# Two pairs of each FFN as plain block products, prompt values by pairs of heads, and raw weights issued ahead of past loads

## The chip, the cores and the metric

One core of a Trainium2 chip runs one launch. The metric is device microseconds (us) of that launch. TensorE (PE) multiplies matrices, VectorE (DVE) and ScalarE (ACT) work elementwise, GpSimd (POOL) makes one kind of operand, and SyncE (SP) issues most of the DMAs.

## The reference

One inference step of two layers of a streaming encoder over 640 tokens: 512 of a prompt and 8 sequences of 16 "sample" tokens with 256 cached past rows each. Width 1024, FFN width 2816.

```
for each of the 2 layers (s, b, g come from a conditioning vector, "ada"):
  x += 0.5*(1+g1) * SwiGLU1(rmsnorm(x)*(1+s1)+b1)
  n  = rmsnorm(x)*(1+s2)+b2
  x += (1+g2) * concat(GLA(n @ W_in), MLA(n @ W_in)) @ W_out
  x += 0.5*(1+g3) * SwiGLU2(rmsnorm(x)*(1+s3)+b3)
swiglu(x): a, b = split(x @ w_in); (silu(a) * b) @ w_out
MLA: 8 heads, scores over a low-rank latent of 256 and a rotary key of 32, block-causal softmax, values of 64 per head
```

GLA is gated linear attention of 4 heads. The last step is one more rmsnorm.

## The kernel before

**Arithmetic.** An fp32 operand is split into a high part (a cast to fp32r, on ACT) and the rest (`lo`, a subtraction on DVE or POOL), and a product is three matmul passes: high by high, weight high by token low, weight low by token high. Tokens run in two halves of 320 columns (`cols`). The small matmuls of the attention are plain fp32; each of them shows as two passes in the trace.

**FFN.** Its 2816 hidden columns are 22 *pairs* (128 columns of the gate, 128 of the up matrix), in three portions of 8, 8 and 6 pairs, each followed by its part of the output matrix (`ffn`, PE L1050). A pair and its tokens are seen as 2x2 blocks (gate or up by input half; input half by token half) and are multiplied by a scheme of **seven block products** in place of eight. One block product (`product`, L1040) is 4 chunks by 3 passes = 12 passes of 320 columns on lines L1045, L1046 and L1047. With two layers of two FFNs there are 4 x 22 pairs x 7 x 12 = 7392 such passes. The scheme needs

- token operands: the blocks B11, B21, B22 of the normed input, and four sums T_1 to T_4 of blocks (`tsum` on DVE), each cast on ACT (`hi`, L600) and subtracted on DVE (`lo`, L1587);
- weight operands: three raw blocks and four sums `s_t`, two made early (`s_in_pair`) and two later (`s_late`, L1722) on DVE, with casts on ACT (`hi_a` to `hi_d`, L519, L534, L524, L529) and `lo` on DVE (`lo_a` to `lo_d`);
- sums of results: copies out of PSUM on ACT (`half_out` L618 with L622, L641, L656) and additions on DVE, with SiLU on ACT.

An FFN starts behind the last residual of the stage before it. Then come, in order: the last squares (`tail` on DVE), the norm's `rstd` with a load of the SiLU table (L577), scaling (`scaled`, DVE) and bias (L596, ACT), the casts and residuals of B11 and B21, the four sums with theirs, and B22. The function is `norm_hi_t` (L589) on ACT and `norm_apply_t` (L1562) on DVE. The weights of the first pair are prepared ahead of this by `first_hi` and `first_lo`.

**Mixer.** `mix_pe` (L1126), `mix_act` (L694), `mix_dve` (L1804). Its 28 + 8 weight units of 512 KB come through two `raw` buffers, are cast by `feed(k)` on ACT (L695, cast L514) into four `w_hi` slots, and POOL makes `w_lo` (L479). The attention is one software-pipelined loop of 40 steps: 8 sample steps (one sequence each), then 32 prompt steps (8 heads by 4 query tiles `qt`, head by head). A step is: scores (PE L1429), a maximum (DVE L2092), an exponential (ACT L926 and, for samples, L928), a normalisation (DVE L2106), transposes (PE L1441), a copy out of PSUM (ACT), values (`values`, L1444: PE L1458 for samples, L1468 for the prompt). Prompt values of one head are 64 output rows; even heads fill rows 0 to 63 of a bank, odd heads rows 64 to 127. L1486 multiplies the sample latents by `w_uv`, 64 rows per head.

**What sets the order.** Every engine has its own program written out in order; engines meet only at semaphores. ACT waits for a raw unit's DMA inside `feed`; SP issues the units in order, each when `w_lo` of an earlier unit is done, and puts the loads of past keys and values (`load_past`, L410) between them at unit `U_UV`.

Of the kernel before, what the change touches and what calls it, by code (L numbers as in the profile page):

```python
# [11 lines left out]
P = 128  # L12
# [17 lines left out]
WPL = 6 * DC + MIX_U  # L30
# [17 lines left out]
B11, B21, T_2, T_1, T_3, T_4, B22 = range(7)  # L48
# [28 lines left out]
def build(nc, xT, cT, lng, bada, fing, selc, wmain, wada, scanm, gk2_in, gains_in, tri_in, bd_in, seqm_in,  # L77
          ident_in, qmask_in, kmask_in, cs_in, ukT, wuv_in, past_kT, past_v, past_pe, s0_in,
          y_out, ckv_out, kpe_out, glap_out, glas_out):
    with ExitStack() as ctx:  # L80
# [60 lines left out]
        t_hi = [sb(f"t_hi{i}", [P, 4, HALF], F32R, at=a)[0] for i, a in enumerate(tok_at)]  # L141
        t_lo = [sb(f"t_lo{i}", [P, 4, HALF], F32R, at=a + 5120)[0] for i, a in enumerate(tok_at)]
        n32 = sb("n32", [P, DC, NT], at=arena_a)[0]
        t_two = sb("t_two", [P, 4, HALF], at=arena_a + 20480)[0]
# [44 lines left out]
        pt_p = [in_a(f"pt_p{i}", [P, 4, P], 30720 + 2048 * i) for i in range(3)]  # L189
# [111 lines left out]
        pv_mm = signal("pv_mm", 32)  # L301
# [76 lines left out]
        def whole(l, f, p, m):  # L378
            return l * WPL + f * (3 * DC + MIX_U) + p * DC + m

        def mixw(l):
            return l * WPL + 3 * DC

# [3 lines left out]
        def pairs_next(l, f, p):  # L387
            return p < 2 or (f == 1 and l + 1 < DEPTH)

        def pair(l, f, p, c):  # L390
            return (l * 2 + f) * NFF + PBASE[p] + c

# [4 lines left out]
        SBANKS, TBANKS = (6, 5, 2, 3), (7, 0)  # L397

# [7 lines left out]
        def _(sp):  # L406
# [34 lines left out]
            for l in range(DEPTH):  # L441
                for f in range(2):
                    for p in range(3):
                        n0, w0 = pair(l, f, p, 0), whole(l, f, p, 0)
                        for c in range(PORT[p]):
                            if f == 0:
                                for k in range(2):
                                    load_ada(4 * ada_block(l, p, c) + 2 * (c % 2) + k, k, 2)
                            sp.wait_ge(s_step, 4 * (n0 + c) + 4)
                            for k in range(2):  # L450
                                load_main(unit(l, f, p, 2 * c + 2 + k))
# [23 lines left out]
        def _(pool):  # L475
# [24 lines left out]
            for l in range(DEPTH):  # L500
                for first, count in ((0, 28), (28, WPL - 28)):
                    if first:
                        norm_samples(l)
                    with pool.Fori(0, count // 4) as i:
# [5 lines left out]
        def _(act):  # L510
# [59 lines left out]
            def norm_rstd(g, s):  # L570
# [5 lines left out]
                if s and g < 3 * DEPTH:  # L576
                    act.preload_act_table_set(WITH_SILU)  # L577
# [11 lines left out]
            def norm_hi_t(g, gi):  # L589

                def bias(i):
                    h, half = i % 2, i // 2
                    c = (slice(0, HALF), slice(HALF, SEQ))[half]
                    act.wait_ge(xr_done, 4 * gi + i + 1)
                    for m in range(4 * h, 4 * h + 4):
                        act.activation(n32[:, m, c], n32[:, m, c], ACT.Identity, bias=mod_b[:, m, 0:1],  # L596
# [4 lines left out]

                act.wait_ge(mab_done, 2 * g + 2)
                for h in range(2):
                    bias(h)
                    act.wait_ge(nb_done, 16 * gi + 4 * h + 4)
                    hi((B11, B21)[h], n32[:, 4 * h:4 * h + 4, cols[0]])
                bias(2)
                bias(3)
                half_out(NFF * gi)
                for i, need, src in ((T_2, 2, t_two[:]), (T_1, 1, n32[:, 0:4, cols[0]]), (T_3, 3, n32[:, 0:4, cols[1]]),  # L610
                                     (T_4, 4, n32[:, 4:8, cols[0]])):
                    act.wait_ge(tsum_done, 4 * gi + need)
                    hi(i, src)
                act.wait_ge(nb_done, 16 * gi + 16)
                act.wait_ge(sam_step, 3 * gi + 3)
                hi(B22, n32[:, 4:8, cols[1]])
# [7 lines left out]
            def ffn(l, f):  # L624
                for p in range(3):
                    n0, w0, last = pair(l, f, p, 0), whole(l, f, p, 0), PORT[p] - 1
                    for c in range(PORT[p]):
                        n = n0 + c
                        if c == 0 and p:
                            half_out(n)  # L630
                        act.wait_ge(p2_mm, n + 1)
                        if c < last:
                            hi_a(n + 1, unit(l, f, p, 2 * c + 2))
                        else:
                            split_hi(w0, unit(l, f, p, 2 * PORT[p]))
                        act.wait_ge(c11_done, n + 1)
                        act.activation(g0[n % 2][:], g0[n % 2][:], ACT.Silu).then_inc(sil_done, 1)
                        act.wait_ge(p6_mm, n + 1)
# [1678 lines left out]
```

## Time and profile before

| | |
|---|---|
| median of 3 runs | 2818.18 us (2817.44 to 2822.74) |
| the profiled execution | 2817.91 us, its span 2815.8 us |
| mean granted TensorE clock in the span | 0.963 |
| PE busy | 2607.1 us, 93% |
| DVE busy | 1588.2 us, 56% |
| ACT busy | 1085.9 us, 39% |
| POOL busy | 407.4 us, 14% |
| DMA | 283.86 MB, mean 101 GB/s |

The span is the time in the trace from the first to the last instruction of the core; 2.1 us of the execution lie outside it. A granted clock of 1.00 is 2.4 GHz and 0.50 is 1.2 GHz. Rows name buffers without their numbers; `<-` stands between outputs and inputs, and the text in brackets at the end of a timeline row is the idle time of the engine just before the instruction and what ended it. A row with `x8` is a run of eight like instructions with their common duration.

### The profile page before, as it was taken

What the parts mean: (1) busy time and instruction counts of PE and PEld (TensorE: products, weight loads), DVE (VectorE), ACT (ScalarE), POOL (GpSimd) and SP (SyncE); (2) the same over time, 40 slices, a digit from 0 to 9 for tenths busy, and PEclk for the clock granted to TensorE, in tenths of its full rate; (3) what the DMA queues carried; (4) which work ended last, traced back from release to release, by engine and by line L of the source; (5) the groups of instructions that cost most, each with busy time, mean ns of one, the idle gap of its engine ahead of it and who ended that gap; (6) DMA issues with size and microseconds to landing.
All of it is one profiled execution on the core that took longest, in us unless ns stands there. A gap on an engine that the chain in (4) does not pass through costs nothing.

```text
span 2815.8 us, 42934 instructions
## 1 busy us (share of the span) xinstructions
PE 2607.1 (93%) x17236; PEld 2417.7 (86%) x17236; DVE 1588.2 (56%) x2712; ACT 1085.9 (39%) x1844; POOL 407.4 (14%) x170
## 2 busy tenths in 40 slices
PE   5799999989889979999979999998998897999997
PEld 1499999989786869999969999998987686999997
DVE  2573655553654476473767466466257437747474
ACT  1342433432444254252454334244334435525242
POOL 0002020233220101102110201114321010020202
PEclk8899999989989989999989999998999998999998
DMA  8543443422240112122224334242215101222222
GB/s 324 211 150 105 135 134 107 135 80 75 71 156 15 33 58 94 58 91 74 98 71 146 119 122 143 98 142 84 87 38 161 51 31 37 92 68 90 76 88 85
DMA packets 81759, 283.86 MB, mean 101 GB/s; under 512 B 10048, under 2 KB 13024, under 8 KB 80928
## 3 DMA queue, kind: packets, MB, share of 16 engines
q1 hardware_dynamic: 75168, 263.81, 27.4%
q10 hardware_dynamic: 6400, 17.37, 2.1%
q8 instruction: 136, 2.23, 0.3%
q14 instruction: 55, 0.45, 0.1%
HBM read 274.69 MB, written 6.46 MB: 100 GB/s over the span
## 4 chain that ended last, share of the span: by engine, by line
issue 69%; PE 20%; POOL 9%; DVE 1%; ACT 1%; POOLq 0%; DMA 0%; DVEq 0%; ACTq 0%
POOL w_lo L479 8%; PE bank L1045 3%; PE bank L1047 3%; PE bank L1046 3%; PE bank L1003 2%; PE bank L1005 2%; PE bank L1004 2%; PE bank L1468 1%; PE bank L1429 1%; PE bank L1458 0%; PE bank L1441 0%; DVE t_lo L1587 0%; DVE y_sb L2173 0%; PE bank L1415 0%; DVE h_lo L1772 0%
## 5 line engine op out<-in xcount | busy, mean ns | idle before, releaser
L1045 PE MATMUL bank<-t_hi,w_hi 128*128 128x320 f32 x2464 | 781.5, 317 | 69.9 <-DVE t_lo L1587 49.8
L1046 PE MATMUL bank<-t_lo,w_hi 128*128 128x320 f32 x2464 | 769.0, 312 | 0.0
L1047 PE MATMUL bank<-t_hi,w_lo 128*128 128x320 f32 x2464 | 768.9, 312 | 0.0
L479 POOL TENSOR_TENSOR w_lo<-raw,w_hi 128x1024 fp32r<-128x1024 f32 x160 | 394.0, 2467 | 2371.2 <-ACT w_hi L514 2371.2
L1045 PEld LDWEIGHTS bank<-t_hi,w_hi 128*128 128x128 f32 x2464 | 469.9, 191 | 118.7 <-issue 60.6
L1046 PEld LDWEIGHTS bank<-t_lo,w_hi 128*128 128x128 f32 x2464 | 470.7, 191 | 0.0
L1047 PEld LDWEIGHTS bank<-t_hi,w_lo 128*128 128x128 f32 x2464 | 470.0, 191 | 0.0
L1003 PE MATMUL bank<-h_hi,w_hi 128*128 128x320 f32 x1408 | 436.3, 310 | 1.4 <-DVE h_lo L1772 1.0
L1004 PE MATMUL bank<-h_lo,w_hi 128*128 128x320 f32 x1408 | 435.1, 309 | 0.0
L1005 PE MATMUL bank<-h_hi,w_lo 128*128 128x320 f32 x1408 | 435.1, 309 | 0.0
L514 ACT CAST w_hi<-raw 128x1024 fp32r<-128x1024 f32 x160 | 166.9, 1047 | 317.3 <-PE bank L1005 283.3
L1003 PEld LDWEIGHTS bank<-h_hi,w_hi 128*128 128x128 f32 x1408 | 264.3, 188 | 3.3 <-DVE h_lo L1772 3.3
L1004 PEld LDWEIGHTS bank<-h_lo,w_hi 128*128 128x128 f32 x1408 | 264.3, 188 | 0.0
L1005 PEld LDWEIGHTS bank<-h_hi,w_lo 128*128 128x128 f32 x1408 | 264.3, 188 | 0.0
L1664 DVE SCALAR_TENSOR_TENSOR x<-bank,mod_g,x 128x192 f32<-128x192 f32 x112 | 46.8, 418 | 283.2 <-PE bank L1005 283.1
L1003 PE MATMUL bank<-n_hi,w_hi 128*128 128x320 f32 x448 | 142.0, 317 | 19.3 <-DVE n_lo L1635 19.3
L524 ACT CAST w_hi<-s_t 128x1024 fp32r<-128x1024 f32 x88 | 92.2, 1048 | 162.4 <-DVE s_t L1714 100.3
L1659 DVE SCALAR_TENSOR_TENSOR x<-bank,mod_g,x 128x320 f32<-128x320 f32 x112 | 61.5, 549 | 151.6 <-PE bank L1005 151.6
L1004 PE MATMUL bank<-n_lo,w_hi 128*128 128x320 f32 x448 | 141.0, 315 | 0.0
L1005 PE MATMUL bank<-n_hi,w_lo 128*128 128x320 f32 x448 | 141.0, 315 | 0.0
L1759 DVE TENSOR_TENSOR up<-up,bank 128x320 f32<-128x320 f32 x88 | 43.0, 488 | 155.6 <-ACT up L656 155.6
L529 ACT CAST w_hi<-s_t 128x1024 fp32r<-128x1024 f32 x88 | 92.4, 1050 | 95.9 <-PE bank L1005 51.4
(263 smaller groups left out, 4103.0 us busy)
## 6 DMA issues: line engine op xcount, KB each, us to landing
raw<-in_wmain SPq DMA_DIRECT2D x336, 512.0 KB, 3.6
araw<-in_wada SPq DMA_DIRECT2D x144, 512.0 KB, 4.6
x<-in_xT SPq DMA_DIRECT2D x1, 2560.0 KB, 15.1
pk_t<-in_pastkT SPq DMA_DIRECT2D x10, 256.0 KB, 4.3
pv<-in_pastv SPq DMA_DIRECT2D x10, 256.0 KB, 5.0
y<-y_sb SPq DMA_DIRECT2D x1, 2560.0 KB, 7.5
s_s<-in_s ACTq DMA_DIRECT2D x4, 512.0 KB, 5.1
uk_t<-in_ukT ACTq DMA_DIRECT2D x2, 1024.0 KB, 6.2
```

Of the source, the lines that this page charges most:

```text
L479: pool.tensor_tensor(w_lo[slot][:], raw[slot % 2][:].rearrange("p (c m) -> p c m", m=P), w_hi[slot][:].bitcast(F32), ALU.subtract).then_in ...
L514: act.copy(w_hi[w % 4][:], raw[at % 2][:].rearrange("p (c m) -> p c m", m=P)).then_inc(whi_done, 1)
L524: act.copy(w_hi[1][:], s_t[:]).then_inc(hib_done, 1)
L529: act.copy(w_hi[3][:], s_t[:]).then_inc(hic_done, 1)
L1003: pe.matmul(out, w_hi[w][:, c, :], r_hi, start=first, stop=False)
L1004: pe.matmul(out, w_hi[w][:, c, :], r_lo, start=False, stop=False)
L1005: return pe.matmul(out, w_lo[w][:, c, :], r_hi, start=False, stop=last)
L1045: pe.matmul(out, hi, t_hi[i][:, c, :], start=first and c == 0, stop=False, skip_group_check=True)
L1046: pe.matmul(out, hi, t_lo[i][:, c, :], start=False, stop=False, skip_group_check=True)
L1047: mm = pe.matmul(out, lo, t_hi[i][:, c, :], start=False, stop=(c == 3), skip_group_check=True)
L1659: dve.scalar_tensor_tensor(out=x[:, m, cols[0]], in0=y0[:, 0:HALF], scalar=mod_g[:, m, 0:1], in1=x[:, m, cols[0]], op0=ALU.mult, op1=ALU.a ...
L1664: dve.scalar_tensor_tensor(out=x[:, m, HALF:SEQ], in0=y1[:, 0:HP1], scalar=mod_g[:, m, 0:1], in1=x[:, m, HALF:SEQ], op0=ALU.mult, op1=ALU.add)
```

## The change

1. **Plain pairs.** `PL = 2`: the first two pairs of each FFN are multiplied as eight block products each (`straight`), first both pairs for tokens 0 to 319, then both for tokens 320 to 639. They take B11, B21, B12 and B22 and raw weights (four units cast by `split_hi`, subtracted by `low_plain`), and no sums. B12 becomes a token block of its own; T_4 lies in B12's place and is cast when the plain products are done. The sums T_1 to T_4 and the operands of the third pair are made while the plain products run. SiLU reads PSUM, and so does the multiplication by the up part (`up_mul`).
2. **Norm.** The SiLU table is loaded behind the cast of B21; `tail(0)` stands ahead of the first scaling.
3. **Feeds and loads.** Of the four units that `feed` cast between the latent queries and the attention loop, two are cast before that, ahead of the `w_uv` step, and two in loop steps 5 and 6. SP issues two more raw units ahead of the past loads.
4. **Prompt values.** The loop takes the heads in pairs, alternating the two heads at each `qt`. `values` runs every second step for both heads, and successive matmuls go to rows 0 to 63 and 64 to 127 in turn; `w_uv` (L1486) alternates in the same way. `pt_p` has four buffers in place of three.

```diff
-B11, B21, T_2, T_1, T_3, T_4, B22 = range(7)
+B11, B21, B12, B22, T_2, T_1, T_3, T_4 = range(8)
+T_HOME = (0, 1, 3, 6, 2, 4, 5, 3)
...
+        def prompt_tile(it):
+            j = it - NDEC
+            return 2 * (j // 8) + j % 2, (j % 8) // 2
...
-                            if k == U_UV:
+                            if k == U_OUT:
                                 sp.wait_ge(gla_st, 64 * l + 64)
                                 load_past(l, (0, 1))
+                            elif k == U_OUT + 1:
                                 sp.wait_ge(wslot_free, mixw(l) + U_UK + 4)
                                 load_past(l, (2, 3, 4))
...
+                act.preload_act_table_set(WITH_SILU)
...
+                silu(1, 1)
+                act.wait_ge(wslot_free, pl + 8)
+                hi_sum(T_4, 4, n32[0][:, 4:8, :])
+                next_hi(2)
+                h_high(1, 1)
+                next_hi(3)
...
+                feed(20)
+                feed(21)
...
-                for k in range(20, 24):
-                    feed(k)
...
+                    if it in (5, 6):
+                        feed(17 + it)
...
+                    if p == 0:
+                        for s in range(2):
+                            for c in range(PL):
+                                straight(c, s, 0)
+                                straight(c, s, 1)
...
+                    if it % 2 == 0:
+                        return
...
                     for k in range(qt + 1):
-                        mm = pe.matmul(bank[(4, 1)[hp % 2]][r0:r0 + MV, qt * P:(qt + 1) * P],
-                                       v_m[:, k, h * MV:(h + 1) * MV], pt_p[it % 3][:, k, :], start=(k == 0), stop=(k == qt))
+                        for e in range(2):
+                            mm = pe.matmul(bank[(4, 1)[hp % 2]][MV * e:MV * e + MV, qt * P:(qt + 1) * P],
+                                           v_m[:, k, (2 * hp + e) * MV:(2 * hp + e + 1) * MV],
+                                           pt_p[(it - 1 + e) % 4][:, k, :], start=(k == 0), stop=(k == qt))
...
-                tail(0)
...
+                dve.wait_ge(nb_done, 16 * gi + 16)
                 tsum(0, n11, n12, n11)
+                up_mul(0, 0)
                 tsum(1, t_two[:], n22, n11)
+                h_low(0, 0)
```

**Order on ACT at the start of the first FFN, before** (`t_hi0` and `t_hi1` are the casts of B11 and B21, `t_hi2` to `t_hi5` of the sums, `t_hi6` of B22; L622 is the copy out of PSUM that the third product waits for):

```order
L577 ACT_TABLE_LOAD
L596 ACTIVATE n32_102<-n32_102,mod_b_75,mod_a_74 128x320 x4
L600 CAST t_hi0_88<-n32_102 128x1280
L596 ACTIVATE n32_102<-n32_102,mod_b_75,mod_a_74 128x320 x4
L600 CAST t_hi1_89<-n32_102 128x1280
L596 ACTIVATE n32_102<-n32_102,mod_b_75,mod_a_74 128x192 x8
L622 COPY g0_0_118<-bank0 128x320
L600 CAST t_hi2_90<-t_two_103 128x1280
L600 CAST t_hi3_91<-n32_102 128x1280
L600 CAST t_hi4_92<-n32_102 128x1280
L600 CAST t_hi5_93<-n32_102 128x1280
L600 CAST t_hi6_94<-n32_102 128x1280
```

and **now** (the end of the plain part on ACT: L639 is SiLU from PSUM, L643 the cast of a finished hidden column, `t_hi7` the cast of T_4, `w_hi0` to `w_hi3` those of the third pair, L685 the copy that was L622):

```order
L639 ACTIVATE g1_0_123<-bank0 128x320
L541 CAST w_hi0_56<-raw0_54 128x1024
L643 CAST h_hi_52<-g1_0_123 128x320
L546 CAST w_hi1_57<-s_t_120 128x1024
L639 ACTIVATE g1_1_124<-bank1 128x320
L622 CAST t_hi7_95<-n32_0_104 128x1280
L556 CAST w_hi2_58<-raw1_55 128x512
L643 CAST h_hi_52<-g1_1_124 128x320
L551 CAST w_hi3_59<-s_t_120 128x1024
L685 COPY g0_0_121<-bank0 128x320
```

The casts of the sums now stand among the SiLUs of the plain pairs, and the copy out of the first product by sevens stands behind the cast of T_4 and both late weight casts.

**Order on ACT at the start of the attention of layer 0, before** (L910 copies the latent queries, L514 are the four feeds, L926 and L928 the first exponential):

```order
L910 COPY q_abs_137<-bank3 128x4x8x16
L514 CAST w_hi0_56<-raw0_54 128x1024
L514 CAST w_hi1_57<-raw1_55 128x1024
L514 CAST w_hi2_58<-raw0_54 128x1024
L514 CAST w_hi3_59<-raw1_55 128x1024
L926 ACTIVATE p_s0_139,psums_85<-bank6,mx_84 128x256
```

and **now** (the same place; L1004 copies transposed scores out of PSUM, L945 and L951 issue loads of past rows):

```order
L971 COPY q_abs_140<-bank3 128x4x8x16
L984 ACTIVATE p_s0_142,psums_85<-bank6,mx_84 128x256
...
L1004 COPY pt_s1_147<-bank0 128x384
L536 CAST w_hi2_58<-raw0_54 128x1024
L951 DMA pv1_193<-in_pastv 128x512
L984 ACTIVATE p_s2_144,psums_85<-bank2,mx_84 128x256
L986 ACTIVATE p_s2_144,psum2_86<-bank2,mx_84 128x16
L1004 COPY pt_s0_146<-bank7 128x384
L536 CAST w_hi3_59<-raw1_55 128x1024
```

No feed stands any longer between the latent queries and the first exponential; two stand behind the copies of steps 5 and 6.

**Order on PE in the prompt attention, before** (L1441 transposes, L1468 values of one head into `bank4`, L1429 scores):

```order
L1441 MATMUL bank7<-ident_82,p_p2_172 128x128 x3
L1468 MATMUL bank4<-pt_p0_147,v_m_136 64x128 x2
L1429 MATMUL bank5<-k_h_167,q_h_166 128x256
```

and **now** (L1544, L1575 and L1532 are the same three):

```order
L1544 MATMUL bank7<-ident_82,p_p0_174 128x128 x3
L1575 MATMUL bank4<-pt_p2_152,v_m_139 64x128
L1575 MATMUL bank4<-pt_p3_153,v_m_139 64x128
L1575 MATMUL bank4<-pt_p2_152,v_m_139 64x128
L1575 MATMUL bank4<-pt_p3_153,v_m_139 64x128
L1532 MATMUL bank3<-k_h_171,q_h_170 128x512
L1544 MATMUL bank0<-ident_82,p_p1_175 128x128 x3
L1532 MATMUL bank6<-k_h_171,q_h_170 128x128
```

Values stand in every second step, twice as many at a time, with `pt_p` of the two heads in turn.

## Rows read from the trace of the kernel before

**Rows 1.** part 1 of the page, the kernel before: busy time of each engine
```profile
PE 2607.1 (93%) x17236; PEld 2417.7 (86%) x17236; DVE 1588.2 (56%) x2712; ACT 1085.9 (39%) x1844; POOL 407.4 (14%) x170
```

**Rows 2.** stretches (start:end, us, busy of PE, PEld, DVE, ACT, POOL, PEclk, DMA, GB/s)
```profile
109.90:152.10 42.20, 36.23 (x216) 33.55 (x217) 36.06 (x42) 24.16 (x38) 0.00 (x0) 0.86 0.30 99
998.40:1041.40 43.00, 33.87 (x193) 32.97 (x194) 35.83 (x41) 24.17 (x38) 0.00 (x0) 0.87 0.12 35
1458.70:1503.60 44.90, 37.24 (x216) 34.56 (x217) 37.31 (x44) 24.19 (x38) 0.00 (x0) 0.84 0.29 93
2350.50:2393.50 43.00, 33.47 (x192) 32.57 (x193) 35.82 (x42) 24.22 (x38) 0.00 (x0) 0.88 0.11 36
```

**Rows 3.** timeline of PE, FFN start 1 (start, duration, operation, [idle before])
```profile
109.92 0.64 PE L1045 MATMUL bank<-t_hi,w_hi 128*128 128x320 f32 x1 [7.92 <-DVE t_lo L1587]
...
113.40 0.63 PE L1045 MATMUL bank<-t_hi,w_hi 128*128 128x320 f32 x1
...
130.76 0.31 PE L1045 MATMUL bank<-t_hi,w_hi 128*128 128x320 f32 x1
...
132.52 0.31 PE L1045 MATMUL bank<-t_hi,w_hi 128*128 128x320 f32 x1
```

**Rows 4.** the stretches again: half speed after one short wait
```profile
1480.30:1483.70 3.40, 3.40 (x14) 3.40 (x14) 2.48 (x5) 1.37 (x2) 0.00 (x0) 0.50 0.01 4
```

**Rows 5.** timeline of DVE, first residual at FFN starts 1 and 2
```profile
108.37 1.49 DVE L1587 TENSOR_TENSOR t_lo<-n,t_hi 128x1280 fp32r<-128x1280 f32 x1
...
996.90 1.49 DVE L1587 TENSOR_TENSOR t_lo<-n,t_hi 128x1280 fp32r<-128x1280 f32 x1 [2.57 <-ACT t_hi L600]
```

**Rows 6.** groups of instructions: count, busy, mean ns, idle before
```profile
L1722 DVE TENSOR_TENSOR s_t<-raw,s_t 128x512 f32<-128x512 f32 x88 | 60.2, 684 | 0.0
...
L622 ACT COPY g<-bank 128x320 f32<-128x320 f32 x88 | 37.4, 425 | 87.6 <-PE bank L1047 87.6
...
L1587 DVE TENSOR_TENSOR t_lo<-n,t_hi 128x1280 fp32r<-128x1280 f32 x24 | 35.0, 1487 | 12.1 <-ACT t_hi L600 12.1
...
L600 ACT CAST t_hi<-n 128x1280 fp32r<-128x1280 f32 x24 | 29.4, 1257 | 8.9 <-DVE n L1592 8.6
```

**Rows 7.** timelines of DVE, ACT and PE, start of the attention, layer 0
```profile
825.98 0.44 DVE L2092 TENSOR_REDUCE mx<-bank 128x1 f32<-128x272 f32 x1 [2.54 <-PE bank L1422]
...
830.79 1.04 ACT L514 CAST w_hi<-raw 128x1024 fp32r<-128x1024 f32 x1 [5.17 <-DMA raw<-in_wmain]
...
834.34 0.47 ACT L926 ACTIVATE p_s<-bank,mx 128x256 f32<-128x256 f32 x1
...
837.57 0.69 PE L1441 MATMUL bank<-ident,p_s 128*128 128x128 f32 x2 [7.70 <-DVE p_s L2106]
```

**Rows 8.** who waited for whom: us in total, times, longest
```profile
PE bank L1441 <- DVE p_s L2106: 15.2, 2, 7.7
```

**Rows 9.** the stretches again: after the wait at the attention's start
```profile
831.70:845.40 13.70, 7.83 (x31) 7.29 (x32) 4.71 (x14) 4.98 (x20) 4.68 (x2) 0.50 0.52 170
```

**Rows 10.** tile of the past keys, layer 0 (min/median/max, first and last issue)
```profile
L415 SPq DMA_DIRECT2D pk_t<-in_pastkT x5: 328/427/433, 792.1 to 811.2; - x5
...
DMA to landing us min/median/max: 2.6/4.3/6.8
```

**Rows 11.** timeline of PE in the prompt attention
```profile
871.33 2.02 PE L1486 MATMUL bank<-o_lat,w_uv 128*64 128x128 f32 x32
...
898.95 1.09 PE L1468 MATMUL bank<-pt_p,v_m 128*64 128x128 f32 x8
...
902.47 0.55 PE L1441 MATMUL bank<-ident,p_p 128*128 128x128 f32 x3 [0.38 <-DVE p_p L2106]
...
909.94 0.55 PE L1441 MATMUL bank<-ident,p_p 128*128 128x128 f32 x3 [0.38 <-DVE p_p L2106]
```

**Rows 12.** groups of instructions: passes of the prompt values
```profile
L1468 PE MATMUL bank<-pt_p,v_m 128*64 128x128 f32 x320 | 48.3, 282 | 3.2 <-DVE o_lat L2110 3.2
```

**Rows 13.** the stretches again: four rounds of the prompt attention
```profile
882.50:912.40 29.90, 28.38 (x154) 18.02 (x153) 16.09 (x49) 15.07 (x50) 0.00 (x0) 1.00 0.00 1
```

More of the change, by code:

```diff
@@ L443, in _ @@
                     for p in range(3):
-                        n0, w0 = pair(l, f, p, 0), whole(l, f, p, 0)
+                        n0, w0 = seven(l, f, p, 0), whole(l, f, p, 0)
                         for c in range(PORT[p]):
+                            straight = c < first_pair(p)
+                            for k in range(2):
+                                if straight:
+                                    sp.wait_ge(wlo_done, plain(l, f) + 2 * c + k + 1)
+                                    load_main(unit(l, f, p, 2 * c + 2 + k))
                             if f == 0:
@@ L605, in norm_hi_t @@
                     act.wait_ge(nb_done, 16 * gi + 4 * h + 4)
[L606 to L613, printed above, removed]
+                    hi((B11, B21)[h], n32[0][:, 4 * h:4 * h + 4, :])
+                if gi == 0:
+                    for k in range(2, 2 * PL):
+                        split_hi(k, k)
+                act.preload_act_table_set(WITH_SILU)
+                for h in range(2):
+                    bias(2 + h)
                 act.wait_ge(nb_done, 16 * gi + 16)
                 act.wait_ge(sam_step, 3 * gi + 3)
-                hi(B22, n32[:, 4:8, cols[1]])
+                for h in range(2):
+                    hi((B12, B22)[h], n32[1][:, 4 * h:4 * h + 4, :])
+                silu(0, 0)
+                hi_sum(T_2, 2, t_two[:])
+                h_high(0, 0)
+                hi_sum(T_1, 1, n32[0][:, 0:4, :])
+                silu(1, 0)
+                hi_sum(T_3, 3, n32[1][:, 0:4, :])
+                h_high(1, 0)
+                silu(0, 1)
+                next_hi(0)
+                h_high(0, 1)
+                next_hi(1)
+                silu(1, 1)
[4 more added lines that the diff above has]
+                next_hi(3)
             def half_out(k):
@@ L626, in ffn @@
                     n0, w0, last = pair(l, f, p, 0), whole(l, f, p, 0), PORT[p] - 1
-                    for c in range(PORT[p]):
-                        n = n0 + c
-                        if c == 0 and p:
+                    for c in range(first_pair(p), PORT[p]):
+                        n, k = n0 + c, seven(l, f, p, c)
+                        if c == first_pair(p):
                             half_out(n)
@@ L983, in _ @@
                 last_square(0, s, None)
[L984 to L985 removed]
+            for k in range(2):
+                split_hi(k, k)
             for s in range(2):
@@ new lines, in straight @@
+                    def straight(c, s, up):
+                        n, slot = n0 + c, 2 * c + up
+                        b = (BW, BY)[c] if up else BZ[c]
+                        pe.wait_ge(wlo_done, pl + slot + 1)
+                        if s:
+                            if up:
+                                pe.wait_ge(hf0_done, n + 1)
+                            else:
+                                pe.wait_ge(sil_done, 2 * n0 + c + 1)
+                        elif up:
+                            pe.wait_ge(y_free, 4 + 2 * out_tile(l, f, 0, 0))
+                        elif n >= 2:
+                            pe.wait_ge(hf0_done, n - 1)
+                        for h in range(2):
+                            i = ((B11, B21), (B12, B22))[s][h]
+                            if c == 0 and not up:
+                                tokens(i)
+                            mm = product(slot, 4 * h, i, b, h == 0)
+                        mm.then_inc(wslot_free if s else (p2_mm if up else p1_mm), 1)
@@ L1072, in ffn @@
+                    for c in range(first_pair(p), PORT[p]):
+                        n, k = n0 + c, seven(l, f, p, c)
+                        new = p == 0 and c == PL
                         z = BZ[n % 2]
-                        if c == 0:
-                            tokens(B11)
-                            one(n)
-                            tokens(B21)
+                        if c == first_pair(p):
+                            one(c)
                             pe.wait_ge(y_free, 4 + 2 * out_tile(l, f, p, 0))
-                            two(n)
```

355 lines of the change are left out of this document (217 added, 138 removed).

## The prediction

> **What bounds the kernel.** I read the busy times first: PE works 93% of the span and no other engine more than 56% [rows 1]. So a microsecond is won where PE is idle, where its clock is at the lower level, or where it does work it need not do. The stretches around each FFN's start show the first two: 42 to 45 us long, the granted clock on the mean 0.84 to 0.88 [rows 2]. The timeline there shows the pace: a product took 3.48 us at the start (109.92 to 113.40) and 1.76 us later (130.76 to 132.52) [rows 3]: 1.2 and 2.4 GHz. The waits show a third place: PE waits twice, 15.2 us together, for the first normalised scores of the attention [rows 8], and is at half clock behind it [rows 9]. In the prompt attention the clock is full and PE busy for 28.38 of 29.9 us, so there only less PE work, or work that overlaps better, helps [rows 13].
>
> **The sum** is made against the profiled execution, 2817.91 us with a span of 2815.8; that is 0.27 below the median of the runs, which is nothing here (what a measurement of this kernel can tell from no change is about 0.2%, 5.6 us).
>
> **FFN starts.** Each stretch of rows 2 holds 16 products of 12 passes (192 passes; 216 where 24 ada passes run too). At 1.76 they take 28.2 us. The second and fourth stretch take 43.0, an excess of 14.8 each. In the first, PE is idle for 42.20 - 36.23 = 6.0 and loses at most 42.2 x 0.14 = 5.9 by its clock; some idle time counts twice, so I take 11. In the third it is 7.7 and at most 7.2: I take 14. The changed kernel also runs 16 products there, but they stand for two pairs where sevens need 14. So, per start:
>
> - *Removed*: the whole excess (11, 14.8, 14, 14.8), since B11 and B21 suffice for the first eight products and B12 and B22 are wanted only 14 us later.
> - *Earlier start*: DVE waited 2.57 us for the cast of B21 at start 2, not at all at start 1 [rows 5]; all such waits are 12.1 [rows 6]. With the table load behind that cast I take 2.3 at starts 2 to 4 and 0 at start 1.
> - *Added*: two products, 24 passes, 3.5 us at full clock.
> - *Left*: PE still starts at half clock. One beginning as long as the stretch of [rows 4], 3.40, loses 1.7; with the ramp's waits for B21 I take 2.1.
> - *A new wait*. T_4's cast waits for the end E of the plain products. ACT and DVE run in order, so behind it come: cast 1.26, `lo` 1.49, a weight residual and two `s_late` at about 0.68 each, a cast of 128x1024 (1.04 in [rows 7]), the copy out of PSUM 0.43 [rows 6]. That is 6.3, with the semaphores about 6.7. Only then may the third product by sevens start, and PE has two products (3.5) to cover it: **3.2 us** of idle time, 2.4 in the FFNs that have ada work there. The T_3 product then waits some 1.1 (0.2 with ada work), since its SiLU and copy are queued behind a weight cast whose raw unit is issued only after `s_late`.
> - *Clock*: a stretch of 3.40 us at 0.50 [rows 4] followed one short wait in the kernel before. I count one such loss per start for the new waits, 1.5, a little under half of 3.40 since part of it lies in the wait.
>
> Sums: start 1: 11 - 3.5 - 2.1 - 2.4 - 0.2 - 1.5 = 1.3. Start 2 and 4: 14.8 + 2.3 - 3.5 - 2.1 - 3.2 - 1.1 - 1.5 = 5.7. Start 3: 14 + 2.3 - 3.5 - 2.1 - 2.4 - 0.2 - 1.5 = 6.6. Together **19**. Bounds: without new waits and clock loss 19 + 2 x 5.8 + 2 x 4.1 = 39; with twice the idle time and clock loss about -1. I stay at 19, since each link of the chain has a row.
>
> Costed at nothing: the up multiplication and SiLU from PSUM (each has a product's time of 3.5 us or more to its next use); the three subtractions of raw weights that replace `s_t` work (DVE is 56% busy; at FFN 1 two units more are cast inside the norm, where ACT waits for DVE anyway); POOL's work, which is unchanged.
>
> **Start of the attention.** The first maximum is ready at 825.98 + 0.44 = 826.4. ACT could take the exponential then, but is in front of the third and fourth feed: 5.17 us for a raw unit's DMA, the casts, and the exponential starts at 834.34 [rows 7]. That is 7.9 late, and PE's wait for its consumer is 7.70. With no feed there, the wait goes, and nothing else is late: the same engine order reaches the exponential as soon as the maximum is there. Behind the wait stands a stretch of 13.7 us at 0.50 with 7.83 of PE work [rows 9]; at full clock that is 3.9 less. So 7.6 + 3.9 = 11.5 per layer, **23** in two. Bounds: 15 (the clock falls all the same, by the waits of the sample steps) and 25. The two feeds now stand in steps 5 and 6, where their raw units have had several steps to land, and cost ACT 1.04 each beside PE work; if the cast were late, the maximum of the following step would wait a microsecond. SP issues the past loads behind two more raw units. Even if all were issued only at 811.2, where the last one stands now, and took the longest landing, 6.8 [rows 10], they are there at 818.0, ahead of the scores that end at 825.98. So nothing.
>
> **Prompt values in pairs.** Eight passes of one head took 1.09, the last one's own 0.28 counted in: a pitch of 0.115. The 32 passes that go to both column halves took 2.02: a pitch of 0.056 [rows 11, 12]. Two heads need 40 passes per eight steps, so at most 2.4 us are won, 2.2 with the ends of shorter groups. Half as many groups save perhaps 0.4 in ends. Two waits of 0.38 for the normalised scores (902.47 and 909.94, one per period) may go: 0.76. A period of four steps is 7.47 now [rows 11], eight are 14.94. PE's work would be 14.94 - 3.3 = 11.6. The softmax chain of a step then has less time, and with DVE at 16.09 and ACT at 15.07 per 16 steps [rows 13] they are not full, but in-order waits give back some; I take 1.4. 13.0 against 14.94, four times per layer: 7.8, **16** in two. Bounds: 0 (the chain sets the period) and 26. `w_uv` already runs at 0.056: nothing.
>
> 19 + 23 + 16 = 58: **2760 us**, a span near 2757.5.
>
> A rule that speaks against the third part stands in the Trainium skill, page "TensorE: Matmul & The Clock Gate", section "Part 3: Packing small matmuls": a weight load overlaps matmuls in flight only if its row group differs, and two column halves share all rows. By it no pass would overlap the other half's. The page "TensorEngine Tiling (Array Packing)", section "Key Properties", has tiles load and multiply in parallel. The trace, with 0.056 per pass in two halves against 0.115 in one, agrees with the latter so far.
>
> **Rivals.**
>
> (a) *The FFN starts give nothing*: the wait on T_4's chain is longer than I have it (a raw unit that lands late, a clock that stays low), and eats the 19. For it: the chain has seven links on two engines in order. Against: every link has its row. 2779.
>
> (b) *Pairing gives nothing*: the softmax chain bounds the loop, or the halves of two different moving operands don't overlap. For: the PE waits of 0.38 exist already. Against: DVE and ACT are about half idle. 2776.
>
> (c) *Better*: the sums' chain is covered, and no clock loss follows it. 2740.
>
> (d) *Slower: alternating halves serialise*, so that each pass takes its own mean 0.282 [rows 12]. Prompt values: 320 x (0.282 - 0.115) = 53. `w_uv`: 64 x (0.282 - 0.056) = 14. With the 16 lost: 2760 + 83 = 2843. It decides from a pitch at which 42 us (the other two parts) are eaten: (42 - 14)/320 + 0.115, about 0.20. Against: the rows of `w_uv`, where halves change every four passes. This is what the rule of "Part 3: Packing small matmuls" in the Trainium skill's page "TensorE: Matmul & The Clock Gate" would make of the change.
>
> (e) *The feeds are only moved*: the scores of steps 5 and 6 wait for raw units as step 0 did, so that the wait goes on there and only the clock is better: 2760 + 15 = 2775.
>
> **Chances.** Forecast as worked 0.62; (a) 0.11, (b) 0.09, (c) 0.08, (e) 0.04; (d) 0.04; 0.02 for two or more of the first failures together, near no change. The range takes in (a), (b), (e) and (c): 2740 to 2786, where the upper end is (a) and part of a second failure, and leaves out some 0.1 to 0.15. Faster by over 0.2%: all but (d) and the last: 0.93. Within 0.2%: 0.02. Slower: 0.05, (d) and a little.
>
> **What the profile would show.** Right: 7392 + 96 = 7488 product passes; no PE wait of 7.7 on normalised scores, and ACT not waiting on a raw DMA ahead of the first exponential; prompt-value passes at a pitch near 0.056 and a period of eight steps near 13.0; at each FFN start no waits on `t_lo` but the first, and a new one of 2.4 to 3.2 on the copy out of PSUM (L685) with a fall of the clock behind it. Wrong: a pitch above 0.11 or a period above 14.5 (b, d); new waits of 6 us or more behind the plain products (a); a wait on raw units within the sample steps (e).

## The result, and the profile after

The changed kernel takes **2749.04 us** (median of 4 runs, 2740.86 to 2751.49) beside 2820.38 (2817.44 to 2822.74, 4 runs): a ratio of 0.9742, 95% interval 0.9718 to 0.9767. The forecast was 2760, its range 2740 to 2786. The profiled execution took 2751.49 us, its span 2749.7, so the two profiles stand 66.1 us apart; the sums below are made against that.

Part 1 of the page of the changed kernel, to be held against [rows 1]:

```profile
PE 2584.8 (94%) x17332; PEld 2406.6 (88%) x17332; DVE 1545.5 (56%) x2644; ACT 1068.9 (39%) x1808; POOL 407.8 (15%) x170
```

PE has 96 passes more and is still busy 22 us less: the values overlap, and less of the time is at half clock (157 us, for 212). The rest of the 66 us is idle time that has gone. I divide both traces at the same places of the program: the first pass of an FFN, the last pass of its eighth pair, the first pass on `n_hi` (mixer), the first score of the attention and the first pass on `o_hi` (the output projection). A boundary is the start of the pass that it names.

| stretch | before | after | gain |
|---|---|---|---|
| start to the first FFN | 109.92 | 104.12 | 5.8 |
| FFN starts, 8 pairs each | 122.36, 114.59, 125.01, 114.59 | 121.24, 109.67, 121.48, 109.73 | 14.4 |
| ends of FFN 1 and 3 to the mixer's first pass | 53.77, 53.75 | 52.03, 52.02 | 3.5 |
| mixer up to the attention | 227.96, 228.03 | 227.47, 227.52 | 1.0 |
| attention | 106.04, 106.00 | 87.03, 86.91 | 38.1 |
| to the start of FFN 2, 3 and 4 | 68.58, 56.94, 69.21 | 67.90, 53.54, 67.90 | 5.4 |
| all else, the end among it | | | -2.1 |

The last row has a place. From the eighth pair of FFN 4 to the end the changed kernel takes 2.4 more, and PE's waits there are two that the kernel before does not have at that place: 1.11 at 2643.2 (L704, behind a cast that waited 1.28 for its raw unit) and 0.96 at 2690.0 (for `h_lo`). No run tests where they come from.

**FFN starts.** The stretches of the changed kernel (columns as in [rows 2]) from the first pass up to the end of the 18 products ahead of T_2, at starts 1 and 2, and the half-clock stretch behind start 2's new wait:

```profile
104.12:141.70 37.58, 37.58 (x240) 35.27 (x240) 29.16 (x31) 21.05 (x30) 0.00 (x0) 0.93 0.25 85
969.58:1003.18 33.60, 33.60 (x216) 33.09 (x216) 26.27 (x26) 19.56 (x28) 0.00 (x0) 0.95 0.05 17
...
1007.20:1010.60 3.40, 3.40 (x15) 3.40 (x14) 1.24 (x3) 2.22 (x4) 0.00 (x0) 0.50 0.48 195
```

216 passes, 18 products, took 33.60 us with PE busy throughout; before, 16 products took 43.0. Then comes the forecast wait, in the waits of the changed kernel (who waited for whom, us in total, times, longest). The wait on L704 is the one at 2643.2, not at a start.

```profile
PE bank L1107 <- ACT g L685: 9.9, 4, 2.9
...
PE bank L1107 <- ACT g L704: 1.1, 1, 1.1
```

The timelines of ACT and DVE show the chain behind T_4's cast at start 2, link by link as the prediction has it; ACT's 2.74 of waiting is DVE's four links:

```profile
999.70 1.27 ACT L622 CAST t_hi<-n 128x1280 fp32r<-128x1280 f32 x1 [1.62 <-PE bank L1109]
1000.88 0.61 ACT L556 CAST w_hi<-raw 128x512 fp32r<-128x512 f32 x1
1001.40 0.46 ACT L643 CAST h_hi<-g 128x320 fp32r<-128x320 f32 x1
1004.59 1.04 ACT L551 CAST w_hi<-s_t 128x1024 fp32r<-128x1024 f32 x1 [2.74 <-DVE s_t L1867]
1005.54 0.42 ACT L685 COPY g<-bank 128x320 f32<-128x320 f32 x1
```
```profile
1001.01 1.49 DVE L1693 TENSOR_TENSOR t_lo<-n,t_hi 128x1280 fp32r<-128x1280 f32 x1 [0.75 <-ACT t_hi L622]
1002.42 0.69 DVE L1847 TENSOR_TENSOR w_lo<-raw,w_hi 128x512 fp32r<-128x512 f32 x1
1003.21 0.69 DVE L1866 TENSOR_TENSOR s_t<-raw,raw 128x512 f32<-128x512 f32 x1
1003.82 0.68 DVE L1867 TENSOR_TENSOR s_t<-raw,s_t 128x512 f32<-128x512 f32 x1
```

**Attention.** The first exponential of layer 0 is released by DVE's maximum and no longer follows a cast; PE's wait of 7.7 [rows 7, 8] is gone (ACT's timeline, the waits, and PE's timeline of one period):

```profile
817.27 0.47 ACT L984 ACTIVATE p_s<-bank,mx 128x256 f32<-128x256 f32 x1 [2.72 <-DVE mx L2249]
```
```profile
PE bank L1544 <- DVE p_s L2263: 0.6, 2, 0.3
```
```profile
865.96 0.55 PE L1544 MATMUL bank<-ident,p_p 128*128 128x128 f32 x3 [0.90 <-DVE p_p L2263]
866.44 0.66 PE L1575 MATMUL bank<-pt_p,v_m 128*64 128x128 f32 x8
...
869.60 0.66 PE L1544 MATMUL bank<-ident,p_p 128*128 128x128 f32 x4 [0.89 <-DVE p_p L2263]
870.19 0.88 PE L1575 MATMUL bank<-pt_p,v_m 128*64 128x128 f32 x12
...
872.90 1.09 PE L1575 MATMUL bank<-pt_p,v_m 128*64 128x128 f32 x16 [0.25 <-ACT pt_p L1011]
...
879.31 0.55 PE L1544 MATMUL bank<-ident,p_p 128*128 128x128 f32 x3 [0.91 <-DVE p_p L2263]
```

The same 320 passes, which kept PE busy for 48.3 before [rows 12], keep it busy for 24.5, each with the mean of 282 ns that it had:

```profile
L1575 PE MATMUL bank<-pt_p,v_m 128*64 128x128 f32 x320 | 24.5, 282 | 2.5 <-ACT pt_p L1011 2.2
```

Sixteen passes take the 1.09 that eight took in [rows 11]. With the last one's 0.28 taken off that is (1.09 - 0.28) / 15 = 0.054 per pass. A period of eight steps is 879.31 - 865.96 = 13.35, against 2 x 7.47 before; two waits of 0.9 per period, and smaller ones, stand where two of 0.38 were.

**What no step of the prediction had.** The first FFN starts 5.8 us earlier. PE's timeline shows where: its wait for the first `ev` in the prologue was 11.28 before, and is 4.48 now.

```profile
41.55 1.88 PE L1024 MATMUL bank<-sel,ev 128*128 128x9 f32 x8 [11.28 <-DVE ev L1541]
```
```profile
34.70 1.88 PE L1086 MATMUL bank<-sel,ev 128*128 128x9 f32 x8 [4.48 <-DVE ev L1647]
```

DVE's timeline shows what stood ahead of that `ev`, before (the last of the first pair's weight residuals) and now (the two residuals of raw units):

```profile
39.66 1.23 DVE L1697 TENSOR_TENSOR w_lo<-s_t,w_hi 128x1024 fp32r<-128x1024 f32 x1 [1.17 <-ACT w_hi L529]
40.81 0.68 DVE L1541 COPY ev<-bank 128x512 f32<-128x512 f32 x1
```
```profile
31.48 2.56 DVE L1886 TENSOR_TENSOR w_lo<-raw,w_hi 128x1024 fp32r<-128x1024 f32 x2 [0.21 <-ACT w_hi L536]
33.96 0.68 DVE L1647 COPY ev<-bank 128x512 f32<-128x512 f32 x1
```

And at the mixer's start PE waits 4.6 in place of 6.3 for the first `n_lo` (waits, before and after):

```profile
PE bank L1003 <- DVE n_lo L1635: 19.3, 6, 6.3
```
```profile
PE bank L1065 <- DVE n_lo L1780: 14.6, 4, 4.6
```

### The profile page after: what moved, and what is told of

Same layout as the page of the kernel before. It is cut to its first block and busy times, and to the rows that moved or that the text cites. A ratio compares the mean times of both kernels' runs of the same rounds, so it can differ in the third digit from the quotient of the medians.

```text
span 2749.7 us, 42964 instructions
## 1 busy us (share of the span) xinstructions
PE 2584.8 (94%) x17332; PEld 2406.6 (88%) x17332; DVE 1545.5 (56%) x2644; ACT 1068.9 (39%) x1808; POOL 407.8 (15%) x170
## 5 line engine op out<-in xcount | busy, mean ns | idle before, releaser
L1109 PE MATMUL bank<-t_hi,w_lo 128*128 128x320 f32 x2496 | 777.1, 311 | 0.0
L1108 PE MATMUL bank<-t_lo,w_hi 128*128 128x320 f32 x2496 | 776.9, 311 | 0.0
L536 ACT CAST w_hi<-raw 128x1024 fp32r<-128x1024 f32 x176 | 183.3, 1046 | 340.0 <-PE bank L1067 323.5
L546 ACT CAST w_hi<-s_t 128x1024 fp32r<-128x1024 f32 x80 | 83.8, 1048 | 145.7 <-DVE s_t L1859 97.8
L551 ACT CAST w_hi<-s_t 128x1024 fp32r<-128x1024 f32 x80 | 83.9, 1049 | 99.1 <-PE bank L1067 51.4
```

The costliest lines, as they stand in the source:

```text
L536: act.copy(w_hi[w % 4][:], raw[at % 2][:].rearrange("p (c m) -> p c m", m=P)).then_inc(whi_done, 1)
L546: act.copy(w_hi[1][:], s_t[:]).then_inc(hib_done, 1)
L551: act.copy(w_hi[3][:], s_t[:]).then_inc(hic_done, 1)
L1108: pe.matmul(out, hi, t_lo[i][:, c, :], start=False, stop=False, skip_group_check=True)
L1109: mm = pe.matmul(out, lo, t_hi[i][:, c, :], start=False, stop=(c == 3), skip_group_check=True)
```

## The experiments

Eight kernels, seven from the changed one and one from the kernel before. Stretches are those of the table above.

### The attention's parts alone

```diff
 # the kernel before, with:
+ prompt_tile, values by pairs, four pt_p, pv_mm of 16, w_uv in turns
+ feed(20), feed(21) ahead of w_uv; feed(22), feed(23) in steps 5 and 6
+ past loads at U_OUT and U_OUT + 1
```

> The kernel before with parts 3 and 4 of the change alone (feeds and past loads, prompt values in pairs); FFNs, norm and prologue as before. My theory (the parts add up; in the changed kernel's profile the attention is 19 us shorter per layer): 38 us under the kernel before, so about 2780, with FFN starts as before. Rival (the attention gains only because something ahead of it, in the FFN or the mixer's start, hands over earlier): less than 30 us, 2790 or more.

Measured: 2785.95 (2784.03 to 2787.71), ratio 0.9879, 0.9863 to 0.9896. The attention takes 86.88 in both layers, as in the changed kernel, and the FFN starts are the old ones within 1.6 (122.35, 114.55, 123.46, 115.50). The attention alone gives 38.3. The time is 34 less, between the 38 of the theory and the 30 of its rival: two stretches beside the attention grew (from the attention to FFN 2 70.67 for 68.58, the second mixer 230.33 for 228.03), and each has a stretch of 3.4 us at half clock that the kernel before does not have there. So the attention's gain needs nothing of the FFNs, and a little of it is given back. Half the total, 34 of 71, is this; the FFNs, the prologue and the mixer's start are the other half. No run separates, within the FFN starts, the plain pairs from the new order of the norm (part 2).

### The four feeds in front of the loop again

```diff
-                feed(20)
-                feed(21)
...
+                for k in range(20, 24):
+                    feed(k)
                 for it in range(40 + 6):
...
-                    if it in (5, 6):
-                        feed(17 + it)
```

> The changed kernel with all four feeds in front of the attention loop again; SP's order of loads stays the new one. My theory (ACT's in-order wait for raw units ahead of the first exponential cost the 7.6 us and the half clock behind it): PE waits 7 to 8 us for the first normalised scores again in each layer, a stretch of 10 to 14 us at half clock behind it, and the kernel is 20 to 24 us slower than the changed one, about 2771. Rival (the gain came from SP's earlier raw units, which stay): the wait is under 3 us and the kernel within 6 us of the changed one.

Measured: 2766.39 (2764.87 to 2769.11), 17 above the changed kernel. The wait is back, and so is the half clock (waits, and the stretch behind the one in layer 0):

```profile
PE bank L1542 <- DVE p_s L2261: 15.3, 2, 7.7
```
```profile
823.50:837.20 13.70, 8.33 (x32) 7.70 (x33) 4.71 (x14) 4.85 (x19) 4.34 (x2) 0.50 0.48 164
```

ACT again stands 5.04 us in front of a raw unit:

```profile
822.03 1.04 ACT L536 CAST w_hi<-raw 128x1024 fp32r<-128x1024 f32 x1 [5.04 <-DMA raw<-in_wmain]
```

The attention takes 98.25 and 96.05: 11.2 and 9.1 more. The order on ACT is the cause; SP's earlier raw units, which this kernel keeps, do not remove the wait. In layer 1 the half-clock stretch was 6.8 long and not 13.7, which goes with the difference between the two layers. The sum of 20.3 lies in the 20 to 24 expected, the total of 17 does not: among the stretches without an edit, the way to FFN 2 and the start of FFN 3 are 1.5 and 1.8 shorter here.

### One head after the other

```diff
-            return 2 * (j // 8) + j % 2, (j % 8) // 2
+            return j // 4, j % 4
...
-                    if it % 2 == 0:
-                        return
...
-                        for e in range(2):
-                            mm = pe.matmul(bank[...][MV * e:MV * e + MV, ...], ..., pt_p[(it - 1 + e) % 4][:, k, :], ...)
+                        e = h % 2
+                        mm = pe.matmul(bank[...][MV * e:MV * e + MV, ...], ..., pt_p[it % 4][:, k, :], ...)
```

> The changed kernel with the prompt's heads one after the other and values of one head per step, four buffers kept. My theory (overlap of the two column halves): four steps take 7.4 to 7.5 us again, a pass 0.11 in place of 0.054; the kernel is 12 to 16 us slower than the changed one, about 2763. Rival (the period comes from the softmax chain, not from the values): within 4 us of the changed kernel.

Measured: 2766.23 (2757.79 to 2767.32), 17 above the changed kernel. The attention takes 94.90 in both layers, 7.9 and 8.0 more. The rows of four steps are those of [rows 11] again, 877.76 - 870.29 = 7.47 apart:

```profile
870.29 0.55 PE L1544 MATMUL bank<-ident,p_p 128*128 128x128 f32 x3 [0.38 <-DVE p_p L2261]
...
874.24 1.09 PE L1573 MATMUL bank<-pt_p,v_m 128*64 128x128 f32 x8
...
877.76 0.55 PE L1544 MATMUL bank<-ident,p_p 128*128 128x128 f32 x3 [0.38 <-DVE p_p L2261]
```

7.9 here and 11.2 for the feeds make 19.1, the 19.0 that the attention of layer 0 gained: there the two add up. In layer 1 they make 17.1 of 19.1, since the half-clock stretch that came back with the feeds was the shorter one. The medians differ by 17, one more than the 12 to 16 expected; the two profiled executions differ by only 6.3, since this kernel's ran with fewer stretches at half clock (a mean granted clock of 0.976, against 0.972 in its other three). So the 7.9 of the attention is the measure here, and not the total.

### Pairs, but one half's matmuls behind the other's

```diff
-                    for k in range(qt + 1):
-                        for e in range(2):
+                    for e in range(2):
+                        for k in range(qt + 1):
```

> The changed kernel with the values of a pair of heads in another order: all of one head's matmuls, then all of the other's, in place of turns. Theory A (halves overlap only if neighbours in the order go to different halves): a group of 16 passes takes 1.5 to 1.7 us in place of 1.09, and the period of eight steps grows by 1 to 2 us. Theory B (a run of one half can run ahead beside the other's, as the passes of w_uv did in the kernel before, which changed halves every four passes at 0.056 each): the group of 8 stays at 0.66 to 0.75, that of 16 below 1.3.

One run: 2758.18. Neither theory holds for all lengths (PE's timeline):

```profile
880.81 0.67 PE L1575 MATMUL bank<-pt_p,v_m 128*64 128x128 f32 x8
884.56 1.15 PE L1575 MATMUL bank<-pt_p,v_m 128*64 128x128 f32 x12
887.54 1.58 PE L1575 MATMUL bank<-pt_p,v_m 128*64 128x128 f32 x16 [0.25 <-ACT pt_p L1011]
```

In turns these are 0.66, 0.88 and 1.09. Two runs of 4 passes overlap as fully as turns do; of two runs of 6 or 8 only a part lies side by side. A period is 14.10 (13.35 in turns), 0.75 more and not the 1 to 2 of theory A. The attention takes 89.80 and 89.68, 2.8 more in each layer: of the 7.9 that pairing gives, 2.8 come from the turns. PE's busy time on these passes is 48.3 with single heads, 30.6 here and 24.5 in turns.

### A longer prologue

```diff
+            dve.wait_ge(whi_done, 1)
+            for k in range(5):
+                dve.tensor_tensor(s_t[:], raw[0][:]..., w_hi[0][:].bitcast(F32), ALU.subtract).then_inc(put_back, 1)
+                dve.wait_ge(put_back, k + 1)
             for k in range(2):
                 low_plain(k)
```

> The changed kernel with five more subtractions of 128x1024 on DVE ahead of the two weight residuals of the prologue, into a buffer that is free there (about 6.5 us of work that nobody needs). My theory (the 5.8 us that the first FFN starts earlier come from the three weight residuals, four sums and two waits that DVE no longer does ahead of the first ada result): PE's wait for that result grows from 4.5 to about 11 us, the first FFN starts 5 to 6.5 us later, and the kernel is 5 to 6.5 us slower, about 2755. Rival (the ada weights' loads set the prologue's end): the start stays within 1.5 us.

Measured: 2753.01 (2748.54 to 2756.16). PE's wait is long again, and the first FFN starts at 108.78, 4.7 later:

```profile
40.41 1.88 PE L1087 MATMUL bank<-sel,ev 128*128 128x9 f32 x8 [10.77 <-DVE ev L1648]
```

That is a little under the 5 to 6.5 expected, and far from the rival's 1.5: by the place where the FFN starts the mechanism holds. In the six kernels that have this prologue and no edit in it, the changed one among them, that place lies between 102.46 and 104.12. The medians lie 4.0 apart, which is less than either kernel's own spread, so the total alone would not have told.

### The cast behind the second rstd again

```diff
                                 last_square(g, 1, out_tile(l, f, 2, m))
+                                if f == 0:
+                                    norm_rstd(g, 1)
...
-                    if p == 2:
+                    if p == 2 and f == 1:
                         norm_rstd(g, 1)
```

> The changed kernel with the cast of a raw unit on ACT behind the second half's rstd and the table load at the mixer's start again, as in the kernel before, in place of ahead of it. My theory (that place delays the mixer's first operand): PE's wait for the first n_lo grows from 4.6 to 6.3 us in each layer, the half-clock stretch from 13.7 to 17.1, and the kernel is 4 to 6 us slower, about 2754. Rival (other parts of the FFN's end shorten that wait): within 1.5 us.

Measured: 2754.81 (2754.12 to 2755.69), 5.8 above. The waits read as in the kernel before:

```profile
PE bank L1067 <- DVE n_lo L1782: 19.3, 6, 6.3
```

The end of the FFN up to the mixer takes 54.39 (52.03), and the mixer up to the attention 230.49 (227.47). The half-clock stretch there is 20.5 us long, not the 17.1 expected, and one more of 3.4 follows at 659.8, which goes with the longer mixer. In the two layers these stretches make 10.7. The medians lie 5.8 apart and the two profiled executions 2.6, since stretches without an edit are some 8 shorter in this one (the FFN starts 3.5, the ways to FFN 2 and 4 2.9, the prologue 1.7). One cast of 1.04 us, put ahead of a wait that ACT had anyway, was worth the 4.7 in the ends of the FFNs; the rest goes with the clock.

### The late links ahead of T_4's cast

```diff
                 silu(1, 1)
-                act.wait_ge(wslot_free, pl + 8)
-                hi_sum(T_4, 4, n32[0][:, 4:8, :])
                 next_hi(2)
-                h_high(1, 1)
                 next_hi(3)
+                half_out(n0 + PL)
+                hi_sum(T_4, 4, n32[0][:, 4:8, :])
+                h_high(1, 1)
...
                 next_lo(1)
+                next_lo(2)
                 up_mul(1, 1)
...
+                next_lo(3)
                 lo(T_4, n21)
-                next_lo(2)
                 h_low(1, 1)
-                next_lo(3)
```

> The changed kernel with another order at the end of the plain products: the half cast of the third pair's up block and its two late sums ahead of the end of the plain products, then the other late cast, then the copy out of PSUM that the third product by sevens waits for, and only then the cast of T_4. My theory (the waits of 2.0 and 2.9 us at the third product come from the chain behind T_4's cast, and each brings 3.4 us at half clock): the four waits (9.9 us together) fall under 0.5 each, the four stretches at half clock behind them go (1.5 to 1.7 each), and the kernel is 12 to 16 us faster than the changed one, about 2735. Rival (the copy waits for its product, not for the order ahead of it): the waits stay over 1.5 us and the time is within 4 us of the changed kernel.

Measured: 2730.01 (2729.13 to 2731.21), ratio to the kernel before 0.9679, 0.9663 to 0.9695; 19 under the changed kernel. No wait on L685 is left among the waits, and the list of half-clock stretches has none behind a plain part. The eight pairs take 117.82, 106.22, 117.89 and 105.27: 3.4, 3.5, 3.6 and 4.5 less, 14.9 together, within the 12 to 16. Of this the waits are 9.9; the rest goes with the clock and depends on the execution: beside the eight pairs of the kernel with the cast behind the second `rstd`, which has the same waits but only one half-clock stretch behind them, it is 11.5. The two profiled executions lie 20.9 apart. The other 6 us lie in stretches that were not edited (the ways to FFN 2 and 4 1.5 shorter each, the mixers 1.6 and 1.7), where this execution has fewer stretches at half clock; why these fall elsewhere I have not tried.

### And the prologue's residuals later

```diff
-            for k in range(2):
-                low_plain(k)
-            with dve.Fori(1, ADA_PRO) as i:
+            ada_pair(1)
+            low_plain(0)
+            ada_pair(2)
+            low_plain(1)
+            with dve.Fori(3, ADA_PRO) as i:
```

> The order of t2_order and, in the prologue, the two weight residuals on DVE one after the second and one after the third pair of ada blocks in place of ahead of them. If the prologue is set by DVE's work ahead of the first ada result: the first FFN starts 2 to 2.5 us earlier than in the changed kernel and the kernel is 2 us faster than t2_order, about 14 to 18 us faster than the changed one, 2733. Rival (the residuals only push the later ada results): the start moves by less than 1 us, 2735.

Measured: **2726.66** (2726.29 to 2728.97, 5 runs), ratio 0.9667, 0.9654 to 0.968: the fastest of all, by some 3 us. PE's wait for the first `ev` falls to 1.80, 2.7 less than in the run before it:

```profile
31.34 1.06 PE L1086 MATMUL bank<-sel,ev 128*128 128x9 f32 x8 [1.80 <-DVE ev L1647]
```

The first FFN starts at 98.62, 4.8 earlier, not 2 to 2.5. The rest goes with the clock: the same eight passes took 1.88 there and 1.06 here, since PE's half-clock time in the prologue's front part was 13.6 us in place of 23.9. The kernel with the cast behind the second `rstd` fits that: its prologue is the unedited one with a wait of 4.47, but with 17.1 us at half clock, and its first FFN starts at 102.46, where the others with that prologue have 103.41 to 104.12. That I had not counted.

## Why the prediction was right

Direction, range and the three mechanisms held; the forecast was 58 us where the profiles stand 66 and the medians 71 apart. That the sum is near is in part luck: terms with errors of 1 to 4 us cancel, and gains that no term had are in the total. By its steps:

- **FFN starts, 19 forecast, 19.8 measured** (14.4 within the eight pairs, 5.4 ahead of them; forecast 12.4 and 6.9). With the way to each start the four gained 1.1, 5.6, 6.9 and 6.2, for 1.3, 5.7, 6.6 and 5.7. The links of T_4's chain have the lengths that were read from [rows 6]; at start 2 the chain took 6.3 from the cast's start to the copy's end, for 6.7, and the waits came out at 2.0 and 2.9 for 2.4 and 3.2. The wait at T_3 that I priced at 1.1 and 0.2 did not come. These two terms were 3.9 too dear and the rest of the sum some 3 too generous, so the total hides errors. Behind each wait stands a half-clock stretch of 3.4 us, like [rows 4], so the clock term came four times; in the profiles of the five other kernels that keep these waits it came 10 times of 20. That the order of these links is the cause of the waits was shown by moving them: 15 us.
- **"Earlier start", 6.9 forecast, 5.4 measured, for a reason that was half of it.** The 2.57 of [rows 5] is DVE's wait for the cast of B11, not of B21, and I laid its end to the table load alone. At start 3, where DVE waited 3.06, the load of 1.28 went from ACT's chain, and the second `rstd` stands 1.7 closer to the last square, since DVE adds the last squares (`tail(0)`) ahead of the first scaling of 1.49; the way to that start is 3.40 shorter. That is read from the rows; no run tests it. Those to FFN 2 and 4 are only 0.7 and 1.3 shorter where each has a half-clock stretch of 3.4 at the output projection in this execution; in the runs where it is missing they take 66.4 to 66.9, not 67.9.
- **Start of the attention, 23 forecast, 20.3 measured** by the feeds put back (11.2 and 9.1), with the wait at 7.7 as read. The half-clock part came out smaller in one layer of that kernel (6.8 us, where the kernel before has 13.7 in both); by what the values leave of the attention's 38.1 it is 22.2.
- **Prompt values, 16 forecast, 15.9 measured** by the heads taken apart (7.9 and 8.0). A pass in turns was 0.054 for 0.056. The period was 13.35, not 13.0: the two waits of 0.38 for normalised scores that I let go stayed, and grew to 0.9 each, so the softmax chain gave back 0.4 more than the 1.4 taken. And in the whole attention, 38.1 came of 39.
- **The step that fell short** is "Costed at nothing". It let the raw weights that replace `s_t` work pass as free, because DVE is 56% busy. But the first pair's operands are made in the prologue, where `first_lo` stood on DVE's queue ahead of the first `ev`, and PE waited 11.28 us for that: 5.8 us that no term had. Nor has the prediction a term for the raw unit's cast that changed places with the second `rstd` at the end of FFNs 1 and 3: 3.5 us in the stretch up to the mixer and 1.0 behind. Both rows were in the trace before; I read only the waits at the places where the change has a heading. 58 + 5.8 + 4.5 is 68.3, and 2.1 was lost, at the end of FFN 4 above all.
- **Rivals.** (a) would show waits of 6 us or more behind the plain part, and the longest is 2.9; (e) would show waits on raw units in the sample steps, and ACT's casts in steps 5 and 6 (831.69 and 835.27) follow the copies ahead of them without a wait. (b) fell with the heads taken apart. (d) fell by the 0.054: each pass has its own weights, both halves use the same rows, and 16 passes took 1.09 us. The rule that the Trainium skill gives in "TensorE: Matmul & The Clock Gate", section "Part 3: Packing small matmuls", by which a weight load overlaps matmuls in flight only if its row group differs, does not describe these rows. The Trainium skill's "TensorEngine Tiling (Array Packing)", section "Key Properties", says that different tiles load and multiply in parallel; the rows agree for turns, and less so for long runs of one half (1.58 us for 16 passes). (c) did not come, at 2749 for its 2740, but its condition is worth as much as it says: without the new wait the kernel runs at 2730.

## What to carry to other kernels

When work moves to another kind of operand, follow that operand to every place where it is prepared, the prologue too: an engine busy 56% on average can still be the one that PE waits for there. When a wait on a long chain is accepted, look whether some links can run before the event that starts the chain; here five moved operations (three on ACT, two on DVE) were worth 15 us inside the FFNs, as much as the whole change had won in the eight pairs (14.4). A matmul of 64 output rows is worth placing in turns with one of the other 64: here 7.9 us per layer for pairs, 2.8 of them for the turns. And where two totals differ by less than the runs of one kernel spread, compare the stretch that was edited.

## What the runs showed of the hardware

The two column halves overlap by order: runs of 4 passes in one half (0.67 us for 8 passes) as well as turns (0.66), runs of 8 much less (1.58 for 16 against 1.09).

The same wait does not always lower the clock. The kernel with single heads has the FFN code of the changed one. Its wait at start 1 is the same 2.02 us, but the stretch behind it is at 1.00, and the eight pairs take 119.12 in place of 121.24. The rows are the wait, the stretch behind it, and the changed kernel's own stretch at that place:

```profile
142.45 0.38 PE L1107 MATMUL bank<-t_hi,w_hi 128*128 128x320 f32 x1 [2.02 <-ACT g L685]
```
```profile
142.20:147.40 5.20, 4.95 (x34) 3.95 (x35) 3.08 (x4) 2.36 (x5) 0.00 (x0) 1.00 0.55 192
```
```profile
143.60:147.00 3.40, 3.27 (x12) 3.30 (x13) 1.43 (x3) 1.19 (x2) 0.00 (x0) 0.50 0.77 288
```

Over the six kernels that keep the two lengths of wait (2.0 and 2.9 us), 14 of 24 such waits have a half-clock stretch behind them. A stretch of 3.4 us costs 1.7 where PE is busy throughout, half of its length, and the profiles of the kernels with the plain pairs have 12 to 18 stretches each, of 3.4 us and longer.

The changed kernel has four waits that may bring one, and its runs spread over 10.6 us; the kernels with the waits removed spread over 2.1 and 2.7. But the kernel with the cast behind the second `rstd` keeps the waits and spread over 1.6. What the runs do show is that the spread goes with the clock: the four runs of the changed kernel took 2740.86 at a mean granted clock of 0.975, 2746.68 at 0.974, and 2751.40 and 2751.49 at 0.972. A difference of 0.003 in 2750 us is about 8 us of full clock, by estimate most of the 10.6. Why the clock falls in one execution and not in another stays open.
